# Experts ordered by their load, four of them in two passes with high and low parts side by side

## What is computed

```python
D_MODEL, SEQ, D_FF, N_EXPERTS, TOP_K = 1024, 256, 3584, 8, 2

def _moe(h, router, w_gate_up, w_down):
    logits = (h @ router).astype(jnp.float32)
    top_v, top_i = lax.top_k(logits, TOP_K)
    gates = jax.nn.softmax(top_v, axis=-1)
    gate_full = jnp.sum(one_hot(top_i, N_EXPERTS) * gates[..., None], axis=-2)
    y = jnp.zeros_like(h)
    for e in range(N_EXPERTS):
        y = y + gate_full[..., e:e + 1] * _swiglu(h, w_gate_up[e], w_down[e])
    return y                     # swiglu: (silu(h @ W_g) * (h @ W_u)) @ W_d

# layer 0: pooling mixer (4 + 1 + 4 weight tiles), dense swiglu (42 tiles)
# layer 1: dilated attention (40 tiles), _moe (8 x 42 tiles); then a final RMS norm
```

## Time and profile before

| | us |
|---|---|
| runs | 1636.99, 1640.10, 1640.62 |
| median | 1640.1 |
| profiled execution | 1637.7 |
| its span, first to last instruction | 1635.9 |

### The profile page before, as it was taken

One profiled execution on the slowest core, in us unless ns is written; L12 is line 12 of the kernel. 1 busy time (PEld: TensorE's weight loads), 2 busy tenths in 40 slices (PEclk: granted clock), 3 DMA queues, 4 the chain that ended last, 5 costly groups with the idle time before them and its releaser, 6 DMA issues.

```text
span 1635.9 us, 21671 instructions
## 1 busy us (share of the span) xinstructions
PE 1595.3 (98%) x7918; PEld 1310.8 (80%) x7918; DVE 1193.0 (73%) x980; ACT 1006.3 (62%) x818; POOL 130.2 (8%) x127
## 2 busy tenths in 40 slices
PE   8999999999899988999999999999999999998996
PEld 6888888899799876888888888888888888886885
DVE  4555454454654568888888888888888888886886
ACT  5444343443633466777777777777777777775774
POOL 0000000050323133000000000000000000000000
PEclk9999999999999999999999999999999999999998
DMA  9555555576256516999999999999999999999992
GB/s 338 197 180 180 182 181 187 170 221 216 80 180 207 180 53 229 351 384 355 374 377 351 375 376 351 375 376 351 374 377 351 373 378 351 374 377 320 367 360 83
DMA packets 238077, 468.82 MB, mean 287 GB/s; under 512 B 9744, under 2 KB 15888, under 8 KB 238016
## 3 DMA queue, kind: packets, MB, share of 16 engines
q1 hardware_dynamic: 231504, 453.93, 79.1%
q0 software_dynamic: 3024, 11.01, 2.2%
q10 hardware_dynamic: 3488, 3.06, 0.6%
HBM read 460.60 MB, written 7.37 MB: 286 GB/s over the span
## 4 chain that ended last, share of the span: by engine, by line
PE 93%; DVE 3%; ACT 1%; issue 1%; DMA 0%; SPq 0%; ACTq 0%; DVEq 0%
PE bY L297 9%; PE bY L299 9%; PE bY L298 9%; PE bU L297 8%; PE bG L297 8%; PE bU L299 8%; PE bU L298 8%; PE bG L299 8%; PE bG L298 8%; PE bS L299 3%; PE bS L298 3%; PE bS L297 3%; PE bT L549 2%; DVE logit L1269 1%; PE bT L299 1%
## 5 line engine op out<-in xcount | busy, mean ns | idle before, releaser
L287 DVE TENSOR_TENSOR wlo<-raw,whi 128x2048 fp32r<-128x2048 f32 x426 | 975.3, 2292 | 357.7 <-ACT whi L281 356.5
L281 ACT ACTIVATE whi<-raw 128x2048 fp32r<-128x2048 f32 x426 | 816.7, 1917 | 463.2 <-PE bY L299 163.7
L297 PE MATMUL bU<-whi,eTh 128*128 128x512 f32 x448 | 182.8, 408 | 4.9 <-DVE wlo L287 4.9
L297 PE MATMUL bG<-whi,eTh 128*128 128x512 f32 x448 | 179.5, 401 | 5.9 <-DVE wlo L287 5.9
L297 PE MATMUL bY<-whi,hTh 128*128 128x512 f32 x448 | 178.9, 399 | 0.0
L299 PE MATMUL bG<-wlo,eTh 128*128 128x512 f32 x448 | 178.4, 398 | 0.0
L298 PE MATMUL bG<-whi,eTl 128*128 128x512 f32 x448 | 178.4, 398 | 0.0
L299 PE MATMUL bU<-wlo,eTh 128*128 128x512 f32 x448 | 178.0, 397 | 0.0
L298 PE MATMUL bU<-whi,eTl 128*128 128x512 f32 x448 | 178.0, 397 | 0.0
L298 PE MATMUL bY<-whi,hTl 128*128 128x512 f32 x448 | 177.6, 396 | 0.0
L299 PE MATMUL bY<-wlo,hTh 128*128 128x512 f32 x448 | 177.5, 396 | 0.0
(11 more groups left out here) (404 smaller groups left out, 2338.3 us busy)
## 6 DMA issues: line engine op xcount, KB each, us to landing
raw<-in_m_w_gate_up_dram SPq DMA_DIRECT2D x224, 1024.0 KB, 6.3
raw<-in_m_w_down_dram SPq DMA_DIRECT2D x112, 1024.0 KB, 5.9
raw<-in_b_w_in_dram SPq DMA_DIRECT2D x36, 1024.0 KB, 5.2
raw<-in_f_w_gate_up_dram SPq DMA_DIRECT2D x28, 1024.0 KB, 5.1
raw<-in_f_w_down_dram SPq DMA_DIRECT2D x14, 1024.0 KB, 5.1
raw<-in_a_w_out_dram SPq DMA_DIRECT2D x4, 1024.0 KB, 16.1
biasrev<-toeplitz SPq DMA_DIRECT2D x32, 128.0 KB, 4.8
raw<-in_b_w_out_dram SPq DMA_DIRECT2D x4, 1024.0 KB, 5.1
```

The source lines that it names most:

```text
L281: nc.scalar.activation(whi[:, t % CUT], raw[:, t % RAW], ACT.Copy).then_inc(hi_done, 1)
L287: nc.vector.tensor_tensor(wlo[:, t % CUT], raw[:, t % RAW], whi[:, t % CUT].bitcast(F32), ALU.subtract).then_inc(lo_done, 1)
L297: pe.matmul(dst, a[0], b[0], start=start, stop=False)
```

## The change

Experts get a new order, a second kind of item, another place for the overflow loop, and matmuls that read and write backward.

- **Order.** Item 0 is expert 0. Experts 1 to 7 are ranked by their number of tokens on the chip (`experts_by_load`), and items 1 to 7 take ranks 0, 4, 1, 5, 2, 6, 3. SP reads an expert's number from SBUF into a register (`value_load`) before its loads. The loop now has 3 turns of two items, one of the lower ranks and one of the higher.
- **Half items** (1, 3, 5, 7; ranks 0 to 3, up to 64 tokens). The 64 tokens' high parts and low parts lie side by side in one 128-wide `eTh`, so a block takes two matmuls, with `whi` and with `wlo`, and a tile 8. Rows 0 to 63 of the bank then hold the high parts' sum and rows 64 to 127 the low parts'. ACT copies both banks G and U; PE adds the halves and turns them in one step, by 8 matmuls of 64 columns with `fold` (two identities one above the other); ACT takes silu of 256 columns, DVE multiplies 256 columns, ACT and DVE split them (256 columns each). The result's two halves are added to memory by two scatters.
- **Full items** (0, 2, 4, 6) are as before.
- **Small DVE work** is spread over the 7 slabs of item 0 (`aside`).
- **Overflow loop** now has 4 turns and stands after the last item, before the last addition to `x` and the norm. Its items load their own weights. The last spread now waits for `yl` before its first matmul.
- **Backward.** All matmuls with 512 moving columns of weights, in both layers and in full and half items, read the columns from the last to the first and write the bank from the last column to the first (`backward`).

The pieces of the diff below are, in this order: the backward access and a dense product with it; PE's half item; PE's order of items; ACT's slab of a half item; DVE's small work, last item and overflow loop.

```diff
+        def backward(t, first, width):
+            return bass.AP(t[:].tensor, first + 511, [[width, P], [-1, 512]])
+        def wblk_backward(t, b):
+            first = t % CUT * 2048 + b * 512
+            return backward(whi, first, CUT * 2048), backward(wlo, first, CUT * 2048)
...
-                            mm = mm3(pe, banks[tb][:], tok(xh, xl, kb, tb), wblk(t0 + n, b),
+                            mm = mm3(pe, backward(banks[tb], 0, 512), tok(xh, xl, kb, tb), wblk_backward(t0 + n, b),
...
+            def half_item(n, k, amid=lambda j: None, late=lambda: None):
+                def product(t, xs, ks, bank, stop):
+                    tile_ready(T_MOE + t, n)
+                    for b, kb in enumerate(ks):
+                        w = wblk_backward(T_MOE + t, b)
+                        pe.matmul(backward(bank, 0, 512), xs[:, kb], w[0], start=kb == 0, stop=False)
+                        mm = pe.matmul(backward(bank, 0, 512), xs[:, kb], w[1], start=False, stop=stop and b == len(ks) - 1)
+                    mm.then_inc(tile_used, 1)
+                def turn_slab(j):
+                    pe.wait_ge(gate_copied, count(k, SLABS, j + 1))
+                    pe.wait_ge(up_copied, count(k, SLABS, j + 1))
+                    if j >= 1:
+                        pe.wait_ge(jt_mul, count(k, SLABS, j))
+                    for part, src in enumerate((msilu, mh)):
+                        for c in range(4):
+                            to = slice(part * 256 + c * HALF_CAP, part * 256 + (c + 1) * HALF_CAP)
+                            mm = pe.matmul(T[:, to], src[:, c * P:c * P + P], fold[:], start=True, stop=True)
+                    mm.then_inc(jt_psum, 1)
...
+            full_item(0, 0, first_amid, lambda: turn_tokens(0))
+            pe.wait_ge(fold_ready, 1)
+            with pe.Fori(0, LOW - 1) as r:
+                half_item((r, 2, 1), (r, 1, 0), **ahead_of((r, 2, 1)))
+                full_item((r, 2, 2), (r, 1, 1), **ahead_of((r, 2, 2)))
+            half_item(E - 1, LOW - 1, last_amid, last_spread)
+            pe.wait_ge(x_added, 1)
+            pe.wait_ge(y_lo, 2)
+            spread(1, (S0, S1))
...
+                for j in range(SLABS):
+                    ahead(4 * j)
+                    act.wait_ge(tile_used, count(n, FFN_TILES, T_MOE + 4 * j + 2))
+                    if j >= 1:
+                        act.wait_ge(jt_psum, count(k, SLABS, j))
+                    copy(msilu, G[:], gate_copied)
+                    if j >= 1:
+                        slab_silu(j - 1)
+                    ahead(4 * j + 1)
+                    ahead(4 * j + 2)
+                    amid(j)
+                    if j >= 1:
+                        slab_hi(j - 1)
+                    act.wait_ge(tile_used, count(n, FFN_TILES, T_MOE + 4 * j + 4))
+                    copy(mh, U[:], up_copied)
+                    ahead(4 * j + 3)
...
+            aside = {0: gates_by_expert, 1: experts_by_load, 2: tables_by_slot, 3: table_of_rows,
+                     4: full_experts, 5: lambda: [overflow(0), overflow(1)], 6: lambda: [overflow(2), overflow(3)]}
+            full_item(0, 0, **routed(0, 48, True), aside=aside)
...
+            half_item(E - 1, LOW - 1, late=last_add, y_cut=functools.partial(y_low, E - 1), alone=True)
             with dve.Fori(0, OVER) as m:
                 with dve.If(m < m_last):
...
-            item_body(m_last + (E - 1), m_last, last=True)
             dve.wait_ge(sc_psum, m_last * 2 + 2)
```

More of the change, by code:

```diff
@@ L67, with count, one, after @@
 PAIRS0 = SLABS * NT
+RANK_OF_SLOT = (-1, 0, LOW, 1, LOW + 1, 2, LOW + 2, 3)
+def count(i, per, plus=0):
+    if isinstance(i, int):
+        return i * per + plus
+    register, step, first = i
+    return register * (step * per) + (first * per + plus)
+def one(i):
+    return slice(i, i + 1) if isinstance(i, int) else bass.ds(count(i, 1), 1)
+def after(i):
+    return i + 1 if isinstance(i, int) else (i[0], i[1], i[2] + 1)
 def encoder(nc, x_in, rel_bias, gains_t, norm_ffn, norm_final, a_w_in, a_w_group, a_scale, a_w_out,
@@ L771, in spread, with full_item @@
+            def spread(h, banks):
+                for part, y in enumerate((yh, yl)):
+                    for tb in (1, 0):
+                        mm = pe.matmul(banks[tb][:], selT[:, tb], y[:, h * 512:h * 512 + 512], start=part == 0, stop=part == 1)
                 mm.then_inc(sc_psum, 1)
-            def item_body(i, m=None, last=False):
-                direct = m is None
-                pe.wait_ge(ga_hi, i * 2 + 1)
-                pe.wait_ge(ga_lo, i * 2 + 1)
+            def full_item(n, k, amid=lambda j: None, late=lambda: None):
@@ L827, in item_body @@
-                if not direct and not last:
-                    spread(1, m * 2 + 1)
-            with pe.Fori(0, E - 1) as i:
-                item_body(i)
-            pe.wait_ge(ids_ready, 1)
+                        if h == 0 and qn == 0:
+                            pe.wait_ge(ht_lo, count(k, SLABS, PAIRS0 + SLABS - 1))
+                        if h == 0 and qn == DT - 1:
+                            pe.wait_ge(ht_lo, count(k, SLABS, PAIRS0 + SLABS))
+                        product(DOWN + DT * h + qn, hTh, hTl, ks, (Y0, Y1)[h], qn == DT - 1)
@@ L1034, in _, with cut_next @@
             cut_tokens(0)
-            def item_body(i, m=None, last=False):
-                direct = m is None
-                nc.scalar.activation(small[:, 10:11], ident[:, 0:1], ACT.Silu)
+            nc.scalar.activation(small[:, 10:11], ident[:, 0:1], ACT.Silu)
+            def cut_next(n, half):
+                for b, bank in enumerate((G, U)):
+                    act.wait_ge(ga_psum, count(n, 2, 5 + b))
+                    if half:
+                        copy(eTh[:, 4 * b:4 * b + 4, 0:HALF_CAP], bank[:].rearrange("p (k t) -> p k t", k=4)[:, :, 0:HALF_CAP],
+                             ga_hi)
+                    else:
+                        copy(eTh[:, 4 * b:4 * b + 4].rearrange("p k t -> p (k t)"), bank[:], ga_hi)
@@ L1340, in _ @@
             link(nc.vector.tensor_tensor(places[:, E:2 * E], Y1[:, E:2 * E], totals[:, 0:E], ALU.add))
-            for tb in range(NT):
-                sl = slice(tb * 8, tb * 8 + 8)
-                last = nc.vector.scalar_tensor_tensor(rank_item[:, tb, 0:E], places[:, sl], SHIFT, chosen[:, sl],
-                                                      ALU.add, ALU.mult)
-            link(last)
-            def pick(n):
+            held, keys, order, caps, off, off2 = (route[:, 8 * i:8 * i + 8] for i in range(6))
@@ L1400, in _ @@
                 for tb in range(NT):
                     sl = slice(tb * 8, tb * 8 + 8)
-                    picks += [(over_place[:, sl], rank_item[:, tb, E + n:E + n + 1]),
-                              (gate_item[:, tb, 1:E + 1], gate_item[:, tb, E + n + 1:E + n + 2])]
+                    last = nc.vector.tensor_scalar(scrap[:, tb], first[:, sl], gates[:, 2 + tb:3 + tb], None, ALU.mult)
+                link(last)
+                for tb in range(NT):
+                    sl = slice(tb * 8, tb * 8 + 8)
+                    nc.vector.scalar_tensor_tensor(gates_of[:, sl], second[:, sl], gates[:, 4 + tb:5 + tb],
+                                                   scrap[:, tb], ALU.mult, ALU.add)
@@ L1473, in item_body @@
                 for t in range(DOWN, FFN_TILES):
-                    if t == FFN_TILES - 1 and not direct:
+                    if t == FFN_TILES - 1:
                         y_cut(1)
```

599 lines of the change are left out of this document (383 added, 216 removed).

## The result

The changed kernel takes **1623.3 us**, the median of 5 runs (1621.7 to 1628.5), beside 1639.7 us (1637.0 to 1640.6) of the kernel before. The ratio is 0.991, 95% interval [0.989, 0.993]: 16 us faster, where 61 were forecast. It lies 15 us outside the range. The profiled execution took 1621.7 us, its span 1619.8.

A forecast was written before the change was run, and what follows sets the result against it. PE was taken to bound each item at 122.7 us, with the DMA next at 116.1. 1637.7 - 52.0 - 3.0 - 8.5 + 2.5 = 1576.7 us profiled, so 1579 us as median; range 1530 to 1608.

The forecast's parts named there:

- What bounds the kernel before: Limits of one item, in order: PE 122.7 us, DMA 116.1, DVE 105.7, ACT 90.7.
- Half items, 109.7 us: Each of four half items: slabs 74.9, down tiles 31.8 and 3 us more, 13.0 less than before; 52.0 us saved.
- half items gain less: Rival, chance 0.14: one more wait per slab or a slower DMA, half item 116.7 us, total 1607.
- the dearest bound 11.7: Upper bound for a half item's slab, today's 4 x 2.92 us; the cheapest was 10.2, and 10.7 was taken.
- The DMA's lead: Loads about 10 us ahead at item start; a half item uses 6.4, a full item returns 6.6, so it never ends.
- Full items, 122.7, and SP at no cost: Full items unchanged at 122.7 us, 0 us gained; SP's reading of three expert numbers hidden behind loads in flight.
- Item 0, net -3.0: Stall at 633 and half clock save 6.3 us; DVE's small work spread inside item 0 costs 3.3.
- Overflow loop, -8.5 and +2.5: Old place before the last item saves 8.5 us; new place before the last addition costs 2.5.
- Backward, 0: Matmuls of 512 columns read and written backward: 0 us, spacing staying at 0.234 us.
- both rivals on it: Backward faster, chance 0.25, 1537 us; backward slower, chance 0.06, about 2780 us at POOL's factor.
- The faster one: Rival, chance 0.25: backward matmuls of 512 columns start 0.214 us apart, total 1537 us.
- The clock: Rival, chance 0.02: clock falls in half items as PE waits 0.6 us a tile, half item about 152 us, total 1750.

The follow-up runs named there:

- e_all: Changed kernel with four edits: wait per down tile, split before copy of G, loop written out on PE, ACT and DVE, rows matmul in slab 4: 1594.0 us.
- e_down: Changed kernel with PE in half items waiting before each down tile only for the hidden slab it reads, not for slab 5: 1607.4 us, ratio 0.982.
- e_order: Changed kernel with ACT splitting tile 4j+4 before copying G, and DVE its low part before product th, in half items: 1608.7 us, ratio 0.982.
- e_fold: Changed kernel with copies of G, U and the fold matrix as F32R, leaving out low parts of G and U: 1608.1 us, ratio 0.980.
- e_unroll3: Changed kernel with the loop over three pairs of items written out as straight code on PE, ACT and DVE: 1610.9 us, ratio 0.983.
- e_all_sp: e_all with SP's loop over the pairs written out as well: 1587.0 us, ratio 0.968 to the kernel before.
- e_tail: e_all_sp with DVE's overflow loop inside one branch taken only if an expert overflows: 1585.5 us, ratio 0.968 to the kernel before.
- e_rows: Changed kernel with PE's rows matmul of item 0 and its wait for the table moved from slab 3 to slab 4: 1618.0 us, ratio 0.987.
- e_bytes: e_all_sp with half of the half items' weights not loaded, all PE, ACT and DVE instructions kept: 1554.8 us, ratio 0.949 to the kernel before.
- e_forward: Changed kernel with every backward matmul written forward again: 1620.1 us, ratio 0.988 to the kernel before.
- e_unroll: Changed kernel with the loop over three pairs of items written out as straight code on PE alone: 1626.5 us, ratio 0.993.

## Why the prediction was wrong

The sign, and the order of what bounds an item before, were right. The size was off by a factor of nearly 4. By its own steps:

- **What bounds the kernel before**: right. Taking PE's work away did shorten the items, and with the half items' waits removed the next limit was the DMA at 384 to 387 GB/s, as the order of limits had it. The Trainium skill's 358 GB/s (SBUF — State Buffer, section "A bandwidth-pool intuition that's wrong (but worth ruling out)") stays below what the traces show (383 as the mean of 115 us in e_all).
- **Half items, 109.7 us**: the step that failed. They took 116.6, 123.6 and 122.3 us, 33.4 over, and 30.6 with what the full items gave back. I summed DVE's work and added half a microsecond a slab for hand-overs, having followed a slab with the folds at 8 x 0.11. It was the rival "half items gain less" (one more wait per slab than I found), but past its 1607 us. What the runs put in its place: (a) 4.4 us before the down product and the clock behind them, 5.0 us an item in the table (e_down); the sum has no term for the start of the down product, which costs nothing in a full item, where a tile is 12 x 0.234 = 2.8 us of matmuls that cover DVE's order, and here it is 8 x 0.234 = 1.9; (b) the round of a slab through PE, ACT and DVE, in which ACT waits with the split for a fold that takes 1.75 us and not 0.9: slabs of 11.15, between my 10.7 and the dearest bound 11.7, and 5.5 us an item back by ACT's order (e_order) or 4.9 by the fold (e_fold); (c) the branches back, 5.3 us per turn after the first (e_unroll3: 10.7 over two), which the sum put at nothing. The down tiles' 31.8 us are no product of the rows either: 14 x 2.23 are 31.2, half a microsecond less.
- **The DMA's lead**: wrong in its size, but hidden in the result. In the changed kernel ACT never waits for a load in a half item. Once the engines are quick, it does in every half item after the first (e_order, e_all). 45.0 MB at 387 GB/s are 116.3 us; e_all_sp takes 117.3 an item in the mean. I had added 10 us of lead, and had it returned by every full item. The 697.3 us that I forecast for six items are the full rate without a dip, which no run with all the bytes reached; e_all_sp and e_tail, the quickest of them, come to 704.0, and with half the bytes it is 679.0. So of the 30.6 us missing 24 went with the waits, and 7 are left where ACT waits for loads.
- **Full items, 122.7, and SP at no cost**: the first is right to 2 us (120.9 to 122.3 between blocks in the changed kernel). The second is right for the changed kernel, where ACT never waits for a load, and wrong beyond it: 5.0 us in the six items of e_all.
- **Item 0, net -3.0**: failed by 7.8 us. The work inside the item was sized well enough (5.0 us against 3.3, from e_rows). Not followed was one wait: PE's rows matmul for item 0 in slab 3 needs the table that DVE builds in the same slab behind a low part that needs PE. That is 6.1 us with the clock.
- **Overflow loop, -8.5 and +2.5**: the tail grew by 4.3 us from PE's last weight matmul to the last addition (2.6 before, 6.9 after), not by 2.5: the passage on DVE was 5.15 us, near the upper bound 6.2 and not near ACT's 0.5. The -8.5 at the old place can't be read alone, as a half item now stands there. Of the 6.6 us missing, 1.8 are the tail's. The other 4.8 lie in the last item, but they are not one wait's: without its wait before the down product the rest falls by 1.4 us only (e_down), where ACT waits 9.3 us for loads instead, and with half the bytes it falls by 9.9 (e_bytes against e_all_sp). The rest also differs by up to 2.5 us between profiles of kernels with the same last item (142.3 in the changed one, 144.8 in e_forward and e_unroll). How the 4.8 divide is open.
- **Backward, 0**: right, within about 0.3%, and so is the rejection of both rivals on it, to which I had given 0.31. The faster one cost the range its lower end for nothing.
- **The clock**: the rival was out in its form (the clock did not stay down), but its counter-argument did not carry over. In the kernel before, the clock fell only after 4.9 and 5.9 us of idleness; here it fell after gaps of 4.4 and 3.2, and at 1010 to 1014 after one of 2.6. By the estimate above the eight stretches lose some 12 us in all; in the sum they were nothing.

## What to carry to other kernels

When the busiest engine gets lighter, every wait that its queue used to cover comes out: follow each wait of the item, not one slab, with the new time that covers it. Ask for each in-order engine what stands ahead of the instruction that releases another, and whether the wait asks for more than the next instruction reads. A longer loop body can make the branch back dear (0.2 to 0.4 us over one item, 5.4 to 6.7 over two, on three of four engines here), so look at each engine's; taking one away only shows the next.

## What the runs showed of the hardware

- A branch back over two items of code took 6.7 us on PE, 5.4 on ACT and on SP and 0.3 on DVE, and left PE idle for 2.8 and ACT for 3.2 us; over one item, in the kernel before, it took 0.2 to 0.4 us on each. Four empty turns of a loop took DVE 5.15 us in one program and 2.59 in another with the same loop but other code ahead; most of the difference is in the first branch (3.0 and 0.6 us), each further turn took some 0.7. With the three pairs as straight code (e_unroll3) none of PE's waits is put down to "issue".
- A matmul of plain float32 with 64 columns appears as two records of 0.11 us, in F32R as one. The transposes of plain float32, 128 columns, appear as one each (224 for 56 slabs in the kernel before).
- TensorE's granted clock fell to half behind gaps of 4.4 and 3.2 us (starts 4.4 and 3.2 us apart), and behind a gap of 2.6 where others had come shortly before. The length of one gap doesn't decide it: in e_all it fell once in the six items, behind a gap of 2.4, and not behind one of 2.5; in e_tail it fell behind one of 2.2.
- With a column step of -1 in output and moving operand matmuls start 0.23 us apart, as with +1.
